# Seven block products for 24 chunks of the last feed-forward's first layer, and the DRAM-side weight sums placed anew

## The reference

```python
h = rms_norm(x, pre_mlp_g[l])
m = jnp.square(jax.nn.relu(h @ mlp_w1[l])) @ mlp_w2[l]
x = x + rms_norm(m, post_mlp_g[l])
```

## Time and profile before

| | us |
|---|---|
| median of three runs | 1242.89 |
| profiled execution | 1241.57 |
| its span, from the first to the last instruction | 1239.8 |
| TensorE busy | 1231.8 |
| VectorE busy | 852.6 |
| ScalarE busy | 627.4 |

### The profile page before, as it was taken

The page is one execution under the profiler, slowest core; times in us unless marked ns, Lnnn a source line. Parts: engine busy times, 40 slices in busy tenths (PEclk is TensorE's granted clock), DMA queues, the critical chain, the costliest instruction groups (busy, mean ns, idle before and its releaser), DMA issues.

```text
span 1239.8 us, 16100 instructions
## 1 busy us (share of the span) xinstructions
PE 1231.8 (99%) x6230; PEld 1036.1 (84%) x6230; DVE 852.6 (69%) x1227; ACT 627.4 (51%) x1050; POOL 39.6 (3%) x56
## 2 busy tenths in 40 slices
PE   9999999999999999999999999999999999999998
PEld 9877898898889888888888898778898888888886
DVE  5878878576577656665688588887574444487886
ACT  5665654254446444444566464568343332355664
POOL 0000001000000000000000000000000000000000
PEclk9999999999999999999999999999999999999999
DMA  8345445422236686675775337456578676266562
GB/s 294 131 152 201 140 137 170 153 69 85 85 102 204 204 189 203 184 195 198 186 255 187 102 114 218 167 130 158 187 218 207 209 193 163 98 207 200 171 208 98
DMA packets 57925, 209.88 MB, mean 169 GB/s; under 512 B 6228, under 2 KB 13908, under 8 KB 51448
## 3 DMA queue, kind: packets, MB, share of 16 engines
q1 hardware_dynamic: 50504, 158.11, 38.8%
q0 software_dynamic: 6912, 50.33, 16.7%
q10 hardware_dynamic: 432, 0.39, 0.1%
HBM read 200.95 MB, written 56.10 MB: 207 GB/s over the span
## 4 chain that ended last, share of the span: by engine, by line
PE 87%; DVE 1%; ACT 1%; issue 0%; DVEq 0%
PE bank L1424 16%; PE bank L1425 16%; PE bank L1426 16%; PE bank L1630 6%; PE bank L1629 6%; PE bank L1628 6%; PE bank L1569 2%; PE bank L1573 2%; PE bank L1568 2%; PE bank L1571 2%; PE bank L1570 2%; PE bank L1572 2%; PE bank L1679 1%; PE bank L1549 1%; PE bank L1548 1%; PE bank L1547 1%
## 5 line engine op out<-in xcount | busy, mean ns | idle before, releaser
L1424 PE MATMUL bank<-xh,whi 128*128 128x512 f32 (+1 forms) x1136 | 414.2, 365 | 0.8 <-DVE R L2591 0.5
L1425 PE MATMUL bank<-xl,whi 128*128 128x512 f32 (+1 forms) x1136 | 410.4, 361 | 0.0
L1426 PE MATMUL bank<-xh,wlo 128*128 128x512 f32 (+1 forms) x1136 | 410.3, 361 | 0.0
L2356 DVE TENSOR_TENSOR wlo<-stage,whi 128x1024 fp32r<-128x1024 f32 (+1 forms) x258 | 311.2, 1212 | 105.3 <-ACT whi L1862 104.1
L1862 ACT CAST whi<-stage 128x1024 fp32r<-128x1024 f32 (+1 forms) x258 | 266.3, 1039 | 69.2 <-PE bank L1630 29.2
L1424 PEld LDWEIGHTS bank<-xh,whi 128*128 128x128 f32 x1136 | 214.5, 189 | 38.5 <-issue 5.5
L1426 PEld LDWEIGHTS bank<-xh,wlo 128*128 128x128 f32 x1136 | 214.5, 189 | 32.8
L1425 PEld LDWEIGHTS bank<-xl,whi 128*128 128x128 f32 x1136 | 214.6, 189 | 31.8 <-issue 0.2
L1629 PE MATMUL bank<-wlo,xh 128*128 128x512 f32 x328 | 127.7, 389 | 0.0
L1630 PE MATMUL bank<-whi,xl 128*128 128x512 f32 x328 | 127.7, 389 | 0.0
L1628 PE MATMUL bank<-whi,xh 128*128 128x512 f32 x328 | 127.7, 389 | 0.0
(11 more groups left out here) (387 smaller groups left out, 1577.6 us busy)
## 6 DMA issues: line engine op xcount, KB each, us to landing
stage<-in_W_m SPq DMA_DIRECT2D x56, 512.0 KB, 4.2
stage<-in_W_up SPq DMA_DIRECT2D x44, 512.0 KB, 4.1
stage<-in_W_in_a SPq DMA_DIRECT2D x19, 512.0 KB, 3.6
stage<-in_W_down SPq DMA_DIRECT2D x18, 512.0 KB, 4.1
stage<-in_W_out SPq DMA_DIRECT2D x16, 512.0 KB, 4.0
m_a<-in_W_m POOLq DMA_DIRECT2D x8, 1024.0 KB, 7.9
m_b<-in_W_m POOLq DMA_DIRECT2D x8, 1024.0 KB, 8.1
stage<-in_W_in_b SPq DMA_DIRECT2D x10, 512.0 KB, 5.1
```

Of the source, the lines that this page charges most:

```text
L1424: e.matmul(b[:, cols], hi[:, k, :], xh[:, k, cols], start=(k == 0), stop=False)
L1425: e.matmul(b[:, cols], hi[:, k, :], xl[:, k, cols], start=False, stop=False)
L1426: last = e.matmul(b[:, cols], lo[:, k, :], xh[:, k, cols], start=False, stop=(k == 7))
L2356: e.tensor_tensor(wlo[:, plan.place[i], c], stage[:, i % NSTAGE, c], whi[:, plan.place[i], c].bitcast(F32), ALU.subtract).then_inc(S["w_lo"])
```

## The change

- Of the 32 chunks of `m1` the first 8 stay as they are (`PLAIN`). The other 24, six groups of four, become 42 block products (seven for each group), each with a chunk of weights of its own: K is halved to 512, the features are two tiles of 128, and the tokens are 256. A block product is 24 matmuls of 256 columns (`seven_feat`).
- The sums on the token side are made once from an unsplit copy of the turned activations: `raw` (16 KB in each partition), which ScalarE writes at the last boundary (`keep_raw` and one copy more in `moved`). The sums of r1, r2 and r3 take three of the places for split weights from chunk 3 of `m1` on (`keep`), and give them back at the end of `m1`.
- Each group has a sequence of its own (`m1_seven`): r2, t11, r1, r3, t12, r4, t22, with copies and sums between the banks on ScalarE and VectorE.
- The weight sums of `m1` are made in DRAM as for the other two layers: the transfers of GpSimd's queue are now 72 (16 for `down`, 24 for `m1`, 32 for `m2`; the change's own short description speaks of 80). `at(n)` places them anew: eight in the mLSTM part, between the heads' powers; one after; eight from `xq` on; 33 in `up`, one every 1.2 chunks; 18 in the `in2` chunks; four in `m1`.
- NSPLIT goes from 6 to 7; the tile `more` is gone, and its four sums lie in other places.
- In the mLSTM part the four products of a head come first and their statistics after; one load (`mem_load`) is issued a little later.

```diff
-NSTAGE, NSPLIT = 4, 6
+NSTAGE, NSPLIT = 4, 7
...
-           ("out2", 8), ("m1", 32), ("m2", 56)]
+           ("out2", 8), ("m1", 50), ("m2", 56)]
...
-GROUPS = {"down": 4, "m2": 8}
+GROUPS = {"down": 4, "m1": 6, "m2": 8}
+PLAIN = 8
...
+M1_KINDS = ("r2", "t11", "r1", "r3", "t12", "r4", "t22")
+M1_SEVEN = [(kind, PLAIN // 4 + g) for g in range(GROUPS["m1"]) for kind in M1_KINDS]
...
+            if name == "out2":
+                self.raw += 1
+                self.out((name, "turn", t, g), "x_lo", self.x, "raw", self.raw)
...
+            if t == 3:
+                self.step("keep_raw", 1)
         for o in range(3):
             if o == 2:
                 self.turn(name, 3)
+                self.step("keep_raw", 2)
             self.half(name, o)
+        self.step("keep_raw", 3)
...
+    def m1_seven(self, i, kind, g):
+        if kind in ("r2", "t11", "r1", "r3"):
+            self.fill("m1", g, kind)
+        self.need()
+        self.step("seven_feat", i)
+        self.used += 1
+        if kind in ("r1", "r2", "r3") and g == NF2 // 4 - 1:
+            self.give(kind, "mm", CHUNK0["m1"] + PLAIN + i + 1)
+        if kind == "r2":
+            self.copy("m1", "taken", g)
+            self.step("m1_taken", g)
+            if g == PLAIN // 4:
+                self.step("x_sum", "r4")
+                self.x_split("m1", "r4")
+            if g == PLAIN // 4 + 1:
+                self.seven_first("m2")
+        elif kind == "t11":
+            self.combine("m1", "v", g)
+        elif kind == "r1":
+            self.combine("m1", "w", g)
+            self.out(("m1", g, "r1"), "combined", self.combined)
+            self.copy("m1", "seed", g)
+            self.step("m1_seed", g)
+        elif kind == "r3":
+            self.combine("m1", "c22", g)
+            self.combine("m1", "c21", g)
+            self.step("m1_last", g)
+        else:
+            if (kind, g) == ("t22", NF2 // 4 - 1):
+                self.seven_ahead("m2")
+            n = ("t12", "r4", "t22").index(kind)
+            self.step("m1_quarter", n, g)
+            self.out(("m1", g, ("t11", "r2", "r3")[n]), "m1_h", 4 * g + n + 2)
+            if n == 2 and g < NF2 // 4 - 1:
+                self.combine("m2", "r1", g)
+                self.combine("m2", "r3", g)
+        self.pump()
     def mlp(self):
-        for k in self.feat("m1", NF2):
-            if k == NF2 - 1:
-                self.seven_ahead("m2")
+        for k in self.feat("m1", PLAIN):
             self.step("m1", k)
             self.out(("m1", k), "m1_h", k + 1)
-            if k % 4 == 3 and k < NF2 - 1:
+            if k % 4 == 3:
                 self.combine("m2", "r1", k // 4)
                 self.combine("m2", "r3", k // 4)
-            if k == 8:
-                self.seven_first("m2")
-            if 12 <= k < 16:
-                self.step("rms_late", k - 12)
+            if k < 4:
+                self.combine("m1", ("r1", "r3", "r2", "r4")[k])
+            if 3 <= k < 6:
+                kind = ("r2", "r1", "r3")[k - 3]
+                self.keep(kind)
+                self.step("x_sum", kind)
+                self.x_split("m1", kind)
+            if k >= 4:
+                self.step("rms_late", k - 4)
+        for i, (kind, g) in enumerate(M1_SEVEN):
+            self.m1_seven(i, kind, g)
...
+        raw = tiles(reg(64, 4096), 8)
+        X_T = {"t11": (slice(0, 4), slice(0, 256)), "t12": (slice(4, 8), slice(0, 256)),
+               "t21": (slice(0, 4), slice(256, 512)), "t22": (slice(4, 8), slice(256, 512))}
+        SUM_AT = {"r1": "t22", "r3": "t21", "r2": "t11", "r4": "t12"}
...
+            def seven_feat(i):
+                kind, g = M1_SEVEN[i]
+                c = CHUNK0["m1"] + PLAIN + i
+                bank_kind = {"t12": "t11", "r4": "r2", "t22": "r3"}.get(kind, kind)
+                new = kind == bank_kind
+                b = fill("m1", g, kind) if new else bank_of("m1", g, bank_kind)
+                q.wait_ge(S["w_lo"], c + 1)
+                if kind[0] == "r":
+                    q.wait_ge(S["x_lo"], plan.x_at["m1", kind])
+                if kind == "t12":
+                    q.wait_ge(S["combined"], plan.combined_at["m1", "v", g])
+                elif kind == "r4":
+                    q.wait_ge(S["taken"], plan.copied_at["m1", "seed", g])
+                elif kind == "t22":
+                    q.wait_ge(S["combined"], plan.combined_at["m1", "c21", g])
+                hi, lo = (tiles(w[:, plan.place[c], :], 4) for w in (whi, wlo))
+                x, z = m1_x(kind, 0), m1_x(kind, 1)
+                for f in range(2):
+                    o, w = b[:, 256 * f:256 * f + 256], slice(128 * f, 128 * f + 128)
+                    for k in range(4):
+                        e.matmul(o, hi[:, k, w], x[:, k, :], start=(new and f == 0 and k == 0), stop=False, skip_group_check=True)
+                        e.matmul(o, hi[:, k, w], z[:, k, :], start=False, stop=False, skip_group_check=True)
+                        last = e.matmul(o, lo[:, k, w], x[:, k, :], start=False, stop=(k == 3), skip_group_check=True)
+                last.then_inc(S["mm"])
...
+            def keep_raw(t):
+                for g in range(2):
+                    q.wait_ge(S["x_lo"], plan.x_at["out2", "turn", t, g])
+                    e.copy(raw[:, 4 * g:4 * g + 4, tok(t)], tiles(bank_of("out2", "turn", t, g)[:], 4)).then_inc(S["raw"])
             def moved(name, t):
                 q.wait_ge(*tile_ready(name, t))
...
+                src = moved_in[name, t].rearrange("p (b k c) -> p k b c", b=4, k=8)
+                e.copy(xh[:, :, tok(t)].rearrange("p k (b c) -> p k b c", b=4), src).then_inc(S["x_hi"])
+                if name == "out2":
+                    e.copy(raw[:, :, tok(t)].rearrange("p k (b c) -> p k b c", b=4), src).then_inc(own.inc())
+            def x_sum(kind):
+                q.wait_ge(S["combined"], plan.combined_at["m1", kind, 0])
+                if kind == "r4":
+                    q.wait_ge(S["mm"], CHUNK0["m1"] + PLAIN)
+                elif plan.kept[kind][1]:
+                    q.wait_ge(S[plan.kept[kind][1][0]], plan.kept[kind][1][1])
+                e.copy(m1_x(kind, 0), raw_of(SUM_AT[kind])).then_inc(S["x_hi"])
+            def m1_taken(g):
+                q.wait_ge(S["mm"], CHUNK0["m1"] + PLAIN + M1_SEVEN.index(("r2", g)) + 1)
+                e.copy(vs[:, g % 2, :], bank_of("m1", g, "r2")[:]).then_inc(S["taken"])
+            def m1_seed(g):
+                q.wait_ge(S["combined"], plan.combined_at["m1", "w", g])
+                e.copy(bank_of("m1", g, "r2")[:], ws[:, g % 2, :]).then_inc(S["taken"])
+            def m1_quarter(n, g):
+                q.wait_ge(S["mm"], CHUNK0["m1"] + PLAIN + M1_SEVEN.index((("t12", "r4", "t22")[n], g)) + 1)
+                e.activation(t_of("m2", ("t11", "t12", "t21")[n], g), tiles(bank_of("m1", g, ("t11", "r2", "r3")[n])[:], 2),
+                             ACT.Relu).then_inc(S["m1_r"])
...
+                after()
+                for i in range(4):
+                    v = e.tensor_scalar(H[:, tok(i)], b[i // 2][:, (i % 2) * 256:(i % 2) * 256 + 128], dn[:, i:i + 1],
+                                        None, ALU.mult)
+                    v.then_inc(S["ml_n"] if i % 2 else own.inc())
+                q.wait_ge(S["ml_n"], 2 * h + 2)
...
+                    v = e.tensor_tensor(raw_of(SUM_AT[kind]), raw_of(a), raw_of(b), ALU.subtract)
...
+                if kind == "v":
+                    q.wait_ge(S["mm"], done + M1_SEVEN.index(("t11", g)))
+                    q.wait_ge(S["taken"], plan.copied_at["m1", "taken", g])
+                    e.tensor_tensor(v, v, b1, ALU.subtract).then_inc(S["combined"])
+                elif kind == "w":
+                    q.wait_ge(S["mm"], done + M1_SEVEN.index(("r1", g)))
+                    q.wait_ge(S["combined"], plan.combined_at["m1", "v", g])
+                    e.tensor_tensor(w, v, b5, ALU.add).then_inc(S["combined"])
+                elif kind == "c22":
+                    q.wait_ge(S["mm"], done + M1_SEVEN.index(("r3", g)))
+                    q.wait_ge(S["combined"], plan.combined_at["m1", "w", g])
+                    e.tensor_tensor(t_of("m2", "t22", g), tiles(w, 2), tiles(b7, 2), ALU.subtract).then_inc(S["combined"])
+                else:
+                    e.tensor_tensor(b7, b7, v, ALU.subtract).then_inc(S["combined"])
...
+            def at(n):
+                if n < 9:
+                    return CHUNK0["kv_k"]
+                if n < 17:
+                    return CHUNK0["xq"] + n - 8
+                if n < 50:
+                    return CHUNK0["up"] + 2 + 6 * (n - 17) // 5
+                if n < 68:
+                    return CHUNK0["in2_c"] + 1 + (n - 50)
+                if n < 71:
+                    return CHUNK0["m1"] + 3 + 2 * (n - 68)
+                return CHUNK0["m1"] + PLAIN + 2 + 4 * (n - 71)
+            def add_up(lo, hi):
+                for n, (block, part, (name, w), more) in enumerate(ORDER):
```

(20 more changed lines are left out.)

158 lines of the change are left out of this document (94 added, 64 removed).

## The result

The changed kernel takes 1253.64 us, the median of four runs (1250.47 to 1256.92), against 1242.64 for the kernel before on the same chip: 1.0091 times as long, 95% interval [1.0078, 1.0104]. Forecast were 1233.7 us and a range up to 1239.0. The profiled execution took 1256.38 us, with a span of 1254.5 against 1239.8.

What follows compares the result with a forecast made beforehand. TensorE was taken as the bound nearly everywhere, busy 1231.8 of 1239.8 us. Terms -9.6 + 0.9 - 0.5 = -9.2 us gave 1233.7 us from a median of 1242.89; range 1231.3 to 1239.0.

Steps and rivals of the forecast that it cites:

- The sum on TensorE: `m1`: 576 matmuls of 512 columns removed (130.5 us), 1008 of 256 added (121.0 us), difference -9.6 us.
- The choice of 0.120 us for the narrow matmul: New block products in `m1`: a 256-column matmul takes 0.120 us, as at the boundary before; the skill's gap gives 109 ns.
- New work beside it, per block product: `m1` block products: per group of 20.2 us on TensorE, VectorE gets 15.4 us (76%) and ScalarE 10.3 us (51%).
- I cost the stage at nothing: Block-product stage of `m1`: no wait of TensorE, 0 us; upper bound 1.5 us a group, 9 us.
- Within a group: `m1` block products: nearest dependences each have two products, 5.8 us, for two or three operations of 0.7 us.
- I count this as covered: seven places hold 7 x 2.72 = 19 us of work ahead and four buffers more: `down`: some eight transfers beside its 28 block products delay loads without making TensorE wait; up to 13 us if cover goes.
- Rival B: `down`: weights come late beside eight transfers, TensorE stands 13 us, 1246.7 us in all; chance 0.09.
- The signs that the prediction set for being wrong: TensorE waiting for `wlo` in `down` or the new stage, or new lines at 0.109 or 0.125 us.
- The boundary: Last boundary, before `m1`: the raw copy delays tile 2's norm, so tile 3's turn comes 0.9 us late; bounds 0 to +3.
- The six bank copies behind it: Last boundary: copies of 0.5 to 0.6 us delay splits some 3 us, for chunks over 10 us away: nothing.
- The mLSTM term: mLSTM part: a head's four products end about 1.8 us earlier, removing TensorE's 0.5 us wait: -0.5 us.
- The placement elsewhere: Transfers outside `down`: mLSTM powers on time, 18 in `in2` done by 876 to 894 us, `m1` sums ready: no cost.

Runs made afterwards that it cites:

- the best version: Kernel after with m1's plain chunks waiting only for turned tiles, the 33 transfers placed around the boundary before `up`, tile 0's raw copy later: 1231.31 us, ratio 0.9909.
- first experiment: Kernel after, but the plain chunks of `m1` wait only for the last turned tile's `x_lo`, not the newest: 1238.81 us, ratio 0.9969.

## Why the prediction was wrong

**The sum on TensorE was right.** The last stretch of the best version against that of the kernel before is 382.26 - 391.83 = -9.57 us; the prediction had -9.6 for the trade of matmuls. The choice of 0.120 us for the narrow matmul held over 1007 steps. The Trainium skill ("TensorE: Matmul & The Clock Gate", section "Back-to-back issue gap") has a formula that gives 109 ns. But it offers that formula for an isolated matmul and gives measured figures of its own for a stream of weight loads and matmuls, so the prediction used it for what it isn't meant for; no run here shows 109 ns.

**The step that failed first: the new work beside the plain chunks stands in the sum at nothing, without a reason.** "New work beside it, per block product" and "I cost the stage at nothing" are about the block products, which indeed ran without a gap; the making of the sums of tokens before them has no term. The prediction counted the places that they take ("three hold sums of tokens") and looked for dependences only "Within a group". It did not ask who waits for the counter that a new operation raises. The split of each sum raises `x_lo`, and a line the diff doesn't touch waits for the newest value. That turned work that was to lie beside TensorE into a chain: chunk, relu, cast, split, next chunk, 2.9 us a time and 5.1 the first time, where three more sums (L3088, L3090, L3045) stood in front. Cost: 11.4 us of standing and 5.5 of clock, 16.9 together. The three steps stand in the planner's loop (`self.x_split("m1", kind)` in `mlp`); when the loop goes round, `feat` writes the next chunk with the `self.x` that they have raised.

**The second: "I count this as covered: seven places hold 7 x 2.72 = 19 us of work ahead and four buffers more".** Six transfers ran beside `down`, where eight were forecast, and the worst landings were 13.0 us where 9.5 were allowed. Rival B named the place, the transfers and a price of 13 us; the price was 6.8 and the mechanism another. The signs that the prediction set for being wrong (a wait for `wlo`, new lines at 0.109 or 0.125 us) did not come, and it was wrong all the same. The places did cover the weights: no wait for `wlo`. What they cannot cover is an operation queued behind late splits and needed soon, as v is. The head start that counts is that of VectorE's whole queue, not the number of split chunks. The Trainium skill ("DMA: Bandwidth & Descriptors", section "Queues, rings and completion order") has each DMA engine serve its rings in turn, by the packet. The prediction read from it that a load is held up by one packet at a time and that B would all but fall away. But every packet of a load can meet one of the transfer. In the DMA view of 600 to 664 us GpSimd's 1008 packets took 48.9% of the 16 engines' time and the loads' 3063 took 45.2%, so about 0.50 and 0.15 us each: a load that lets one of the other in before each of its own could take some four times as long (an estimate from these rows). The landings lie within that: a median of 7.0 us and up to 13.0 with transfers, 4.1 and 4.8 without. So the rule gave no ground for discounting B.

**The third: the clock.** The prediction priced every stall, rivals included, at its own length. In the kernel after the granted clock fell behind both stops, and 7.9 of the 23.7 us lost went that way (2.4 + 5.5).

**The boundary** (+0.9 forecast, with bounds 0 to 3) measured +0.5 as a wait, and taking the copy away gained 0.9 in the last stretch (383.14 - 382.26). The copy was the cause as argued. The six bank copies behind it, costed at nothing, cost nothing: with the plain chunks freed no wait follows them.

**The mLSTM term** (-0.5) is in line with the interval of the experiment on it (0.1 to 2.2 us less). The -0.5 us of the first stretch say little: with the same mLSTM code `down` began between 612.05 and 613.54 us in the profiles without a new wait ahead of `up`.

**The placement elsewhere** was right: 33 transfers from 387.7 us, the powers on time, the sums in `in2` without cost (82.43 us in both). But they landed 8.3 us apart from 387.7 to 661.4, so 29 of them take 240 us, and `up` lasts 240: there was no room to be off by a few. The prediction took 7.9 us of the earlier trace rows for a plain copy; that row holds copies and accumulating transfers alike. In the trace of the kernel before the 24 copies took 5.2 to 8.7 us (median 6.5), the 24 accumulating ones 7.6 to 11.5 (median 8.9).

What stays open: how much the rows of parameters add to the stop in `down`, why its length differs between versions with the same transfers (2.3 to 4.6 us), and why a stop of 2.3 us came with a drop of the clock and one of 2.9 us without.

## What to carry to other kernels

For each operation that a change adds, look up its semaphore and list every wait on it, in code the diff doesn't touch too; a wait for "the newest value" turns any new producer into a dependence. Count head start in an in-order queue by the operation that is needed soonest, not by the buffers that are full. Transfers of 1 MB in DRAM cost nothing here beside stages whose loads have time to spare; beside a boundary's own small loads they cost about 2 us of waiting, and beside a stage that runs its vector engine at 78% up to 5 us of waiting and the clock on top.

## What the runs showed of the hardware

A stop of TensorE may cost more than its length. In `down` 2.3 us of standing (first experiment) were followed by a granted clock of 0.50, so 1.2 GHz:

```profile
660.00:662.00 2.00, 2.00 (x6) 1.61 (x5) 2.00 (x4) 2.00 (x4) 0.00 (x0) 0.50 0.87 352
```

In the kernel after 4.2 and 5.1 us were too; but 2.9 us by themselves in `m1` left it at 1.00 in the one execution profiled. The length of the stop alone does not tell.

Small loads suffer beside a transfer inside DRAM as large ones do: four of 128 KB went from 2.5 to 7.7 us, chunks of 512 KB from 4.1 to 7.0 in the median. Whether loads slow the transfers in turn isn't shown: the four accumulating ones above, beside `down`'s loads, took 8.3, 10.0, 11.1 and 8.6 us from issue to landing, within the 7.6 to 11.5 us of the kernel before.
